# A two-block transformer kernel on one core: first weight blocks on unnormed inputs, the last squares summed by TensorE, and an attention without a barrier at its entry

## The reference, cut to what matters

```python
h = rmsnorm(h_res, norm1_w); proj = h @ w_in            # q, k, v, z, b_raw, a_raw, ...
qkv = silu(depthwise_conv(concat(q, k, v)))             # 5 taps
q, k = l2norm(q) * dk**-0.5, l2norm(k)
beta = sigmoid(b_raw); g = -exp(A_log) * softplus(a_raw + dt_bias)
o = chunk_gated_delta_rule(...) forwards + backwards
h_res = h_res + merged @ w_out;  h_res = h_res + mlp(rmsnorm(h_res, norm2_w))
```

```python
score = sum_h w_h * relu(qi_h . ki);  idx = top_k(score)   # sparse attention: mask out all others
p = softmax(q . k * scale + mask);    o = p @ v
```

## Time and profile before

| | |
|---|---|
| median of 3 runs | 2712.94 us (2712.76 to 2715.92) |
| the profiled execution, time | 2710.24 us |
| its span, first to last instruction | 2708.5 us |
| TensorE busy | 2593.3 us (96%) |
| VectorE busy | 1446.2 us (53%) |
| ScalarE busy | 989.6 us (37%) |
| GpSimd busy | 1093.0 us (40%) |
| mean granted TensorE clock | 0.988 of full |

### The profile page before, as it was taken

The page is one execution under the profiler, slowest core; times in us unless marked ns, Lnnn a source line. Parts: engine busy times, 40 slices in busy tenths (PEclk is TensorE's granted clock), DMA queues, the critical chain, the costliest instruction groups (busy, mean ns, idle before and its releaser), DMA issues.

```text
span 2708.5 us, 47436 instructions
## 1 busy us (share of the span) xinstructions
PE 2593.3 (96%) x17631; PEld 2256.8 (83%) x17631; DVE 1446.2 (53%) x2090; ACT 989.6 (37%) x1811; POOL 1093.0 (40%) x560
## 2 busy tenths in 40 slices
PE   6999899899999999999898999999999999999999
PEld 5987888878987788887877689999999976788887
DVE  7874767515247642426787547345467234645533
ACT  5655434132222422224243753221243366422222
POOL 4335343244444444445435124444444311444443
PEclk9999999999999999999998999999999999999999
DMA  3223010132222222223211012222222200223222
GB/s 103 79 79 93 13 14 13 38 127 86 93 88 90 96 95 98 93 93 101 71 40 47 2 37 89 87 92 90 89 94 79 79 25 2 93 90 96 93 93 101
DMA packets 88948, 201.82 MB, mean 75 GB/s; under 512 B 36292, under 2 KB 38390, under 8 KB 88800
## 3 DMA queue, kind: packets, MB, share of 16 engines
q1 hardware_dynamic: 82812, 192.19, 22.2%
q10 hardware_dynamic: 5988, 7.58, 0.8%
HBM read 193.81 MB, written 5.92 MB: 74 GB/s over the span
## 4 chain that ended last, share of the span: by engine, by line
issue 46%; PE 29%; POOL 11%; DVE 7%; POOLq 3%; ACT 3%; DVEq 1%; ACTq 0%; SPq 0%; DMA 0%
PE ps L553 20%; POOL wl L517 10%; PE ps L1314 5%; POOLq L2460 2%; DVE work L2363 1%; DVE top L2360 1%; PE ps L1431 1%; PE ps L1430 1%; POOL xbl L2469 1%; PE ps L2123 1%; ACT dec L1573 0%; ACT dec L1566 0%; POOLq L2468 0%; DVE xbh L700 0%; POOLq L130 0%
## 5 line engine op out<-in xcount | busy, mean ns | idle before, releaser
L517 POOL TENSOR_TENSOR wl<-wraw,wh 128x1024 fp32r<-128x1024 f32 x352 | 879.5, 2499 | 1181.4 <-ACT wh L509 1181.4
L509 ACT ACTIVATE wh<-wraw 128x1024 fp32r<-128x1024 f32 x352 | 371.4, 1055 | 517.6 <-PE ps L553 500.3
L553 PE MATMUL ps<-xah,wh 128*128 128x264 f32 (+1 forms) x2656 | 496.6, 328 | 20.3 <-ACT xah L758 7.7
L553 PE MATMUL ps<-xah,wl 128*128 128x264 f32 (+1 forms) x2656 | 487.6, 324 | 0.0
L553 PE MATMUL ps<-xal,wh 128*128 128x264 f32 (+1 forms) x2656 | 485.1, 323 | 0.2 <-DVE xal L745 0.2
L553 PEld LDWEIGHTS ps<-xah,wh 128*128 128x128 f32 x2656 | 403.5, 190 | 75.8 <-issue 21.1
L553 PEld LDWEIGHTS ps<-xah,wl 128*128 128x128 f32 x2656 | 401.9, 189 | 41.0 <-issue 1.0
L553 PEld LDWEIGHTS ps<-xal,wh 128*128 128x128 f32 x2656 | 400.5, 188 | 41.1 <-DVE xal L745 0.5
L707 DVE TENSOR_TENSOR res<-res,stage 128x512 f32 (+3 forms) x112 | 80.4, 718 | 409.9 <-ACT stage L625 409.9
L553 PE MATMUL ps<-xbh,wh 128*128 128x264 f32 (+1 forms) x1392 | 276.7, 337 | 6.5 <-DVE xbl L702 3.6
L553 PE MATMUL ps<-xbl,wh 128*128 128x264 f32 (+1 forms) x1392 | 272.9, 334 | 0.0
(11 more groups left out here) (384 smaller groups left out, 2967.5 us busy)
## 6 DMA issues: line engine op xcount, KB each, us to landing
wraw<-in_w SPq DMA_DIRECT2D x352, 512.0 KB, 3.3
res<-in_x SPq DMA_DIRECT2D x4, 528.0 KB, 5.8
z_out<-stage ACTq DMA_DIRECT2D x8, 256.0 KB, 2.1
z_again<-z_out ACTq DMA_DIRECT2D x1, 2048.0 KB, 9.4
res<-in_x ACTq DMA_DIRECT2D x1, 2048.0 KB, 15.1
out<-res SPq DMA_DIRECT2D x8, 256.0 KB, 4.2
block_out<-yy SPq DMA_DIRECT2D x18, 56.0 KB
block_in<-mt SPq DMA_DIRECT2D x60, 8.0 KB
```

The lines of the kernel that those rows point to most:

```text
L509: act.activation(wh[:, s * DM:(s + 1) * DM], wraw[:, s * DM:(s + 1) * DM], ACT.Copy).then_inc(hi_done, 1)
L517: pool.tensor_tensor(wl[:, s * DM:(s + 1) * DM], wraw[:, s * DM:(s + 1) * DM], wh[:, s * DM:(s + 1) * DM].bitcast(F32), ALU.subtract).then ...
L553: mm = pe.matmul(ps[:, to + h, 0:width], ws[:, s * DM + kk * P:s * DM + (kk + 1) * P], x[:, x0:x0 + width], start=(h not in [o[0] for o in ...
```

## The change: what it does, and the diff

1. **Start.** ScalarE writes the high part of `x * gain` without the norm (`xuh`), VectorE the low part (`xul`); two squares move to GpSimd. TensorE multiplies block 0 tile by tile, with the 8 squares summed by 16 more matmuls between. The loads of the nine constants move from ScalarE's queue to SyncE's, behind the inputs and the first two weight blocks.
2. **Nine unscaled blocks.** Products 0 to 8 of `qkv` use `xuh`, `xul` too, with banks 6, 2, 0 in turn. Each is multiplied by `rstd` as VectorE reads it (`leave(j)`), in place of ScalarE's `cpad` copy. The scaled inputs for the blocks behind are made in the meantime: VectorE scales a tile (`dve_scale`), ScalarE writes the high part, GpSimd the low part, one in each of the first rounds.
3. **Moved in the qkv stage.** Five pieces of the softplus from behind `conv(0)` to `conv(4)` to behind `conv(2)`, 4, 6, 8 and 10; the turns from product 7 to 12; the decay sums from product 9 to 14, and VectorE's work on them from `conv(10)` to `conv(15)`; some memsets behind `conv(9)`.
4. **Norm seams.** The last tile's square isn't added by VectorE: TensorE adds it as a second matmul beside `total`. The sums stand ahead of the second block. The split of that block's weights stands before the last tile's work, and the root's table is loaded early. At the seam with gained squares, the second reciprocal goes behind the first read of an accumulator.
5. **First attention.** No barrier. The first mask is made before the top-k; the others one or two at a time between the first row maxima; a semaphore for each mask, for the turned v and for the rotated q. ScalarE loads the exponential's table early.

```diff
+    def pe_first(pe):
+        def both_halves(ws, x, kk, start=False, stop=False): ...
+        def sums(m): ...            # two matmuls of ones with norm_sq[m], accumulated
+        pe.wait_ge(hi_done, 1)
         for m in range(KT):
+            pe.wait_ge(nfirst, FIRST_COUNT["hi", m])
+            both_halves(wh, xuh, m, start=(m == 0))
+            if m > 1:
+                sums(m - 2)
+        pe.wait_ge(lo_done, 1)
+        for m in range(KT):
+            both_halves(wl, xuh, m)
+        sums(KT - 2)
+        sums(KT - 1).then_inc(nsum, 1)
+        for m in range(KT):
+            pe.wait_ge(nscaled, m + 1)
+            mm = both_halves(wh, xul, m, stop=(m == KT - 1))
...
+    def dve_scale(dve, m):
+        if m >= SCALED:
+            dve.wait_ge(nlo, m - SCALED + 3)
+        dve.scalar_tensor_tensor(scaled[m % SCALED][:, :], tile_at(res, m), gains[:, m:m + 1], rstd[:, :], ALU.mult,
+                                 ALU.mult).then_inc(nscaled, 1)
...
+            if j < UNSCALED:                      # pe_qkv; UNSCALED = 9
+                products(pe, Blk(b, 0), xuh, xul, KT, at=first_bank(b), free=b - 2)
+            else:
+                products(pe, Blk(b, 0), xah, xal, KT, fresh=0 if j == UNSCALED else None)
-            if j == 7:
+            if j == 12:
                 pe_prep_turn(pe)
-            if j == 9:
+            if j == 14:
                 pe_prep_sums(pe)
...
+            if j < UNSCALED:                      # taps(j) in act_qkv: two copies in place of three
+                act.wait_ge(acc_free, num(b) + 1)
...
+            if 1 <= j <= KT:
+                act_scaled_hi(act, j - 1)
-            if j == 8:
+            if j == 13:
                 act_prep_turned(act)
-            if j == 10:
+            if j == 15:
                 act_prep_sums(act)
...
+        def leave(j):
+            b = QKV + j
+            dve.drain()
+            dve.wait_ge(block_done, b + 1)
+            wait(dve, conv_done, j)
+            dve.tensor_tensor(two(cpad[j % 2][:, 2:2 + T]), pair_of(first_bank(b)), two(rstd[:, :]), ALU.mult
+                              ).then_inc(acc_free, 1)
...
         for j in range(24):
+            if j + 1 < UNSCALED:
+                leave(j + 1)
             conv(j)
-            if j < 5:
+            if j + 2 < KT:
+                dve_scale(dve, j + 2)
+            if j in (2, 4, 6, 8, 10):
                 next(decay)
+            if j == UNSCALED:
+                buffers_of_the_first()
-            if j == 10:
+            if j == 15:
                 dve_prep_sums(dve)
...
+            for j in range(24):                   # GpSimd
+                split_lo(pool, Blk(QKV + j + 1, 0))
+                if 1 <= j <= KT:
+                    pool_scaled_low(pool, j - 1)
...
             for h in range(1 if live else 2):     # pe_sums
                 at = off + h * HT
-                mm = pe.matmul(ps[:, 4 + h, 0:width], ones[:, :], total[:, at:at + width], start=True, stop=True)
+                pe.matmul(ps[:, 4 + h, 0:width], ones[:, :], total[:, at:at + width], start=True, stop=False)
+                mm = pe.matmul(ps[:, 4 + h, 0:width], ones[:, :], square[1][:, at:at + width], start=False, stop=True)
...
-            barrier(pe, "pe")                     # and on the three other engines
             pe_attention(pe, False)
...
+        for j in range(2):                        # dve_attention
+            if masks is not None:
+                next(masks)
+            top(j)
+        if masks is not None:
+            next(masks)
```

More of the change, by code:

```diff
@@ L48 @@
 UNITS = HEADS * NCH
+SCALED = 4
+UNSCALED = 9
 NEG = -1.0e30
@@ L352, in build_program @@
     norm_sq = [place(f"norm_sq{m}", [P, T], F32, b_at + m * F) for m in range(KT)]
-    scaled = [place(f"scaled{m}", [P, T], F32, b_at + (KT + m) * F) for m in range(KT)]
+    scaled = [place(f"scaled{i}", [P, T], F32, d_at + 4 * 4 * (T + 8) + i * F) for i in range(SCALED)]
+    assert d_at + 4 * 4 * (T + 8) + SCALED * F <= nc.sbuf_usable_end
+    xuh = place("xuh", [P, KT * T], F32R, phase_at + 16 * TS * 4)
+    xul = place("xul", [P, KT * T], F32R, oacc_at)
     rq = region(phase_at + 17 * F)
@@ L569, in body @@
             elif j == 1:
-                products(pe, b, xh, xl, seg.k, live=live, midway=sums, when=seg.k * (1 if live else 2))
+                products(pe, b, xh, xl, seg.k, live=live, midway=sums, when=0)
             else:
@@ L708, in add_residual @@
         return post
-    def pe_norm(pe):
-        pe.wait_ge(nused, KT - 1)
-        for h in range(2):
-            mm = pe.matmul(ps[:, 4 + h, 0:HT], ones[:, :], norm_sq[0][:, h * HT:(h + 1) * HT], start=True, stop=True)
+    POOL_SQUARES = (0, 1)
+    FIRST_OPS = [("hi", 0), ("hi", 1), ("hi", 2), ("square", 2), ("hi", 3), ("square", 3), ("weights", 0), ("hi", 4),
+                 ("square", 4), ("hi", 5), ("square", 5), ("hi", 6), ("hi", 7), ("square", 6), ("square", 7)]
+    FIRST_COUNT = {op: n + 1 for n, op in enumerate(o for o in FIRST_OPS if o[0] != "weights")}
@@ new lines, in pe_first, with both_halves, sums @@
+    def pe_first(pe):
+        def both_halves(ws, x, kk, start=False, stop=False):
+            for h in range(2):
+                at = kk * T + h * HT
+                mm = pe.matmul(ps[:, first_bank(0) + h, 0:HT], ws[:, kk * P:(kk + 1) * P], x[:, at:at + HT],
+                               start=start, stop=stop)
+            return mm
+        def sums(m):
+            if m in POOL_SQUARES:
+                pe.wait_ge(nsq_pool, POOL_SQUARES.index(m) + 1)
+            else:
+                pe.wait_ge(nfirst, FIRST_COUNT["square", m])
+            for h in range(2):
+                mm = pe.matmul(ps[:, 4 + h, 0:HT], ones[:, :], norm_sq[m][:, h * HT:(h + 1) * HT], start=(m == 0),
+                               stop=(m == KT - 1))
+            return mm
+        pe.wait_ge(hi_done, 1)
[9 more added lines that the diff above has]
+        sums(KT - 1).then_inc(nsum, 1)
@@ L724, in act_norm, with pool_first @@
         norms["act"] += 1
[L725 removed]
+        split_hi(act, Blk(1, 0))
         act.wait_ge(nsum, norms["act"])
         act.activation(two(rstd[:, :]), pair_of(4), ACT.Sqrt, bias=eps[:, 0:1], scale=1.0 / DM).then_inc(nroot, 1)
[L729 to L733 removed]
+    def pool_first(pool):
+        for m in POOL_SQUARES:
+            pool.wait_ge(x_in[m // 2], 16)
+            pool.tensor_tensor(norm_sq[m][:, :], tile_at(res, m), tile_at(res, m), ALU.mult).then_inc(nsq_pool, 1)
@@ L735, in dve_norm, with dve_first @@
+    def dve_first(dve):
+        for m in range(KT):
+            dve.wait_ge(nfirst, FIRST_COUNT["hi", m])
+            dve.scalar_tensor_tensor(tile_of(xul, m), tile_at(res, m), gains[:, m:m + 1], tile_of(xuh, m).bitcast(F32),
+                                     ALU.mult, ALU.subtract).then_inc(nscaled, 1)
     def dve_norm(dve):
@@ L823, in root @@
             dve.drain()
-            if gained:
-                dve.wait_ge(norm_arg, 2)
-                dve.reciprocal(live_stage(0), live_stage(0))
-                dve.drain()
         return root
@@ L2074, in pe_dsa @@
         for j in range(8):
-            products(pe, Blk(a0 + j, 0), xah, xal, KT, **(dict(fresh=2, by_tile=True, when=6 * (KT - 1),
-                                                               midway=pe_sums(live=True, gained=True)) if j == 0 else {}))
+            first = {0: dict(fresh=2, by_tile=True), 1: dict(midway=pe_sums(live=True, gained=True), when=0)}.get(j, {})
+            products(pe, Blk(a0 + j, 0), xah, xal, KT, **first)
             if 2 <= j <= 6:
@@ L2278, in dve_dsa @@
                 dve.tensor_tensor(two(tile_at(pf, 12 + j)), acc(b), two(rstd[:, :]), ALU.mult).then_inc(acc_free, 1)
+                if j == 0:
+                    dve.wait_ge(norm_arg, 2)
+                    dve.reciprocal(live_stage(0), live_stage(0))
+                    dve.drain()
             elif j == 5:
@@ L2328, in dve_dsa @@
         dve.drain()
+        mask(1)
         dve.tensor_tensor(q_scale[:, :, :], q_scale[:, :, :], tok_scale[:, :].unsqueeze(2).broadcast_to([C, NCH, 16]),
                           ALU.mult)
+        dve.drain()
+        yield
+        chosen(2)
+        dve.drain()
+        mask(2)
+        yield
+        for t in range(3, NCH):
+            chosen(t)
+            dve.drain()
+            mask(t)
+        yield
     IX = 2 * (NCH - 1)
@@ L2485, in scores @@
                 pe.wait_ge(f_app, p + 9)
+            if not fox and k == 0:
+                pe.wait_ge(q_done, p + 1)
+            if not fox and j == 0:
+                pe.wait_ge(acc_free, SEGS["dsa_out"].b0)
+            if not fox and j == 1:
+                pe.wait_ge(tok_out, 3)
+            if not fox and p == 0:
+                pe.wait_ge(mask_ready, t + 1)
             q0 = (p + 16 if fox else p) * T + t * C
@@ L3016, in _ @@
             act_dsa(act)
-            barrier(act, "act")
             act_attention(act, False)
```

215 lines of the change are left out of this document (120 added, 95 removed).

## The result

The changed kernel takes 2727.22 us (median of 6 runs, 2724.03 to 2731.05) where the kernel before takes 2713.90 in the same number (2708.02 to 2715.92): a ratio of 1.0053, 95% interval 1.0043 to 1.0064. It is slower by some 14 us. The forecast was 2730.2, with 0.76 on slower. The profiled execution took 2726.71 us, its span is 2724.9, its mean granted clock 0.986. Against the execution of before (2710.24), the one that the sum was made for, it is 16.5 us more; the sum said 17.3.

A forecast was written before the change was run, and what follows sets the result against it. TensorE, 96% busy, was taken to bound the kernel, with VectorE nearly full in the qkv stage. qkv +22.8, plain seams +0.4, gained seam -1.6, attention -4.3 made +17.3 us: 2730.2 from 2712.94, range 2708 to 2744.

The forecast's parts named there:

- The start: Up to qkv's first product: TensorE needs only the first weight split, so block 1 starts at 24.6 us; 14 us gained.
- Products 1 and 2: Early qkv stage: softplus waits behind the norm in ScalarE's queue, so these start 3.1 and 1.7 us late.
- The added VectorE work: qkv rounds 0 to 8: leave 7.0 us, scalings 5.6, contention with GpSimd's low parts 8.4; 21 us in all.
- Nothing left by product 7: qkv stage: at 8.5 us a round, product 3's 7.5 us lead is gone by product 7; product 9 is 3.4 behind.
- The turns: Behind product 12 of qkv: TensorE waits 4.5 us for the last softplus piece, now behind conv(10).
- The first spread: Spread of inverses behind product 16: TensorE waits 8.2 us for VectorE's work on the decay sums, now behind conv(15).
- the walk: Four engine queues stepped in program order at measured durations: first z product at 226.2 us, 22.8 us late.
- The second rival: qkv stage: VectorE lags to product 9, but turns and first spread find their inputs; +1.5 us, 2714; chance 0.12.
- The first rival: qkv stage: added VectorE work falls into idle time, so the kernel gets faster; -13 us, 2700; chance 0.16.
- the third: qkv stage: low parts hold VectorE 1.77 us, each gap over 2 us drops the clock; +23.5, 2736; chance 0.17.
- Seams: Five norm seams: +0.4 us at four plain ones, -1.6 at the gained one, where TensorE still waits 3.5 us.
- The attention's entry: First attention: first exponential sooner after the top-k, masks between the maxima lessen it; -4.3 us, bounds -3 and -5.5.

The follow-up runs named there:

- e3: The changed kernel with the decay preparation moved up and no work added or removed: 2712.75 us, ratio 1.0003 to the kernel before.
- e8: e3 with VectorE's 2.4 us of memsets and copies in round 9 made by GpSimd: 2710.63 us, ratio 0.9997.
- e10: e8 with the norm ready earlier (sums of squares ahead of block 0's products, three scalings and product 1's split moved up): 2703.47 us, ratio 0.9969.
- e5: The kernel before with 14 us of VectorE adds in rounds 0 to 8 and nothing else: 2725.12 us, ratio 1.0051.
- e4: e3 with GpSimd's low parts of the scaled tiles cut from 528 columns to 16: 2710.00 us, ratio 0.9985.
- e1: The kernel before with the norm seams and the first attention's entry changed, without the start and qkv stage: 2703.74 us, ratio 0.9969.
- e11: The kernel before with the norm seams alone changed: 2706.44 us, ratio 0.9984.
- e7: The kernel before with six of the seven multiply-adds of the softplus series left out: 2715.23 us, ratio 1.0008.
- e2: The kernel before with the first attention's entry alone changed: 2705.55 us, ratio 0.9978.

## Why the prediction was right, point by point

- **Direction and sum.** Slower by 16.5 us in the profiled executions, 17.3 forecast. The median, 2727.2, lies 3 us under the forecast and within the range.
- **The start: 14.3 us forecast, 12.5 measured.** The first weights were split at 11.0, not 9.9, and block 1 starts at 26.3, not 24.6. `rstd` is ready at 28.8, forecast 27.1, and VectorE enters the qkv work at 30.2, forecast 28.5. What the forecast passed over is that `rstd` is then later than before (23.4), so that VectorE's first convolution has a lead of 5.8 us and not the 7.8 that the forecast gave its entry.
- **Products 1 and 2.** "3.1 and 1.7 us late" was one wait of 4.1 us and half clock behind it. Product 3 at 49.7, forecast 48.7.
- **The added VectorE work, 21 us forecast: 20.7.** Up to `conv(9)` nine `leave` take 6.4 us, eight scalings 6.1, and the same instructions of convolution and softplus 62.3 instead of 54.1, 8.2 more beside GpSimd's low parts (8.4 forecast). `leave` took 0.71 us in nine of nine cases, eight of them beside GpSimd.
- **Nothing left by product 7.** The lead is 1.5 us at product 7 (80.46 against 82.00). Product 8 starts at 88.20 against 88.67 before, so the lead is used up there; at product 9 the kernel is 1.0 us behind (96.72 against 95.70), not 3.4. `conv(9)` is at 113.4, forecast 112.
- **The turns, 4.5 us forecast: 5.1. The first spread, 8.2: 7.7.** Product 17 at 169.5, forecast 169.2, the first `z` product at 226.30, forecast 226.2. The single errors, the start's among them, partly cancel: 1.7 us too much of a lead at product 0, 2.4 too much of a lag at product 9. That the sum came out to 0.1 us is luck; e3's miss of 7 us shows how good the walk is. The walk was set by two places at which VectorE was late, and missed a third behind them.
- **The share of causes.** The forecast gave 7 us to VectorE's lag and 16 to late stalls. e3 gives 10 of 23 to the order. What remains, 13 us, is VectorE's load, and e8 and e10 brought it back by lightening VectorE and by letting it begin earlier. The forecast priced half clock in this stage at 6 us at most (1.8, 1 and a share of 3); the windows have 11.0 us more of TensorE's busy time for it. One thing was not tested apart: a product now passes from TensorE through VectorE to ScalarE and back to VectorE, and what this longer chain costs beside the added work is open.
- **The second rival** (lag alone, 2714) needed the turns and the first spread to find their inputs. They did not. Its state is what e3 made: 2712.8.
- **The first rival** (added work falls into idle time) is refused by e5, the third (heavier contention) by e4. The third's other condition, that each gap over 2 us drops the clock, does not hold either: three executions kept the full clock behind waits of 2.75 to 2.81 us.
- **Seams: +0.4 at four, -1.6 at the fifth.** The mis-sized term is the gained seam. From the first product's start to the third's it takes 19.45 us (1316.33 to 1335.78) instead of 24.36 (1290.83 to 1315.19): -4.9. The forecast had TensorE wait 3.5 of the 4.9 us, at half clock behind it. It waited 2.8, and the matmuls behind it ran at the full clock, 1.02 us where they had taken 2.04. The wait is the step that was mis-sized. The full clock was this execution's luck: with half clock behind the same wait the seam gains 3.2 (e1, e11). The four others: +1.1 from the first attention's last values to the second's, which holds two of them, then -0.3. Ahead of the gained seam another 2.1 us went (23.4 to 25.5 behind), which the forecast doesn't have. Of these, 1.7 lie between the delta rule's last values and the head norm's first square, and are not the change's: this stretch takes 15.7 us in before and 15.6 in e7, but 17.1 in e2 and 17.0 in e5, where no seam was touched. Why it has two lengths is open.
- **The attention's entry: -4.3 forecast, -5.6 measured** (behind by 21.0 at the top-k's last row, by 15.4 at the first values), just outside the bound of -5.5. The terms listed in the forecast end at 1471.95, not at the 1472.8 that it gives; 0.85 us of it has no name. The chunks behind did not give back what the forecast took for the masks between the maxima.

## What to carry to other kernels

Before an engine's wait at the start is bought off, ask which engine the next stage hangs on: a lead is kept only if that engine gets it, and here the change gave TensorE 12.5 us and VectorE 5.8, and the norm that VectorE needs came 5.4 us later. An engine that is 94% busy in a stage counts as full, even where the engine beside it shows no wait at all; adding to it cost 11 of 14 us, and to take from it brought nothing. A wait costs more than its length: here 24 us more of waiting came with 11 us of half clock. When work is moved past a full stage, price its last use too: preparations put behind the convolutions cost 10 us as stalls that the same work, one or two rounds earlier, did not.

## What the runs showed that was not expected

The delta rule, which the change does not touch, is not of one length. From its first to its last product of values it took 247.1 us in the kernel before, 248.1 after, and 241.6 to 247.7 in the kernels of the experiments. The work is the same; what differs is the granted clock. The windows over this stage, of before and of e5:

```profile
287.00:534.00 247.00, 226.51 (x2218) 217.68 (x2218) 163.47 (x455) 85.89 (x231) 94.66 (x97) 0.95 0.09 14
```
```profile
298.00:540.00 242.00, 219.94 (x2220) 210.85 (x2221) 163.62 (x455) 86.07 (x231) 94.78 (x97) 0.99 0.10 15
```

VectorE, ScalarE and GpSimd are busy for the same time to 0.2 us, TensorE for 6.6 us less at 0.99 than at 0.95 of its clock. So two profiled executions can differ by 6 us for this alone, e4's gain at `z` was not to be seen in its own span for it (its delta rule took 3.0 us more than e3's), and places in a trace ahead of such a stage tell more of a small change than spans do. Why the clock falls in one execution and not in another stays open.

One and the same wait can leave the clock alone or not. At the gained seam nine executions waited 2.75 to 2.81 us behind the same work. In three the next matmuls of 512 columns took 1.02 us for two, as at full clock; in six the clock was at half for part of the sums (1.57 us for two in e1), and the seam took 1.7 us more. Behind the 4.9 us wait of the unchanged seam the clock fell in four of four. What decides it at 2.8 us is not shown, so a gain of this size, read from one trace, should be read again from a second.
